# DMA transposes in place of TensorE transposes for the normalised activations, and the Fourier mixer in its channel-first order

## The reference

```
for l in 0, 1:
    h = rmsnorm(x, mix_norm_g[l])                 # over the 1024 channels of a position
    x = x + (even_mixer if l == 0 else odd_mixer)(h)
    h = rmsnorm(x, ffn_norm_g[l])
    x = x + (silu(h @ w_gate[l]) * (h @ w_up[l])) @ w_down[l]      # 1024 -> 2816 -> 1024
out = rmsnorm(x, final_norm_g)

odd_mixer(h):
    z = h @ w_in                                  # 1024 -> 1536
    c, u, v = z[:512], gelu(z[512:1024]), gelu(z[1024:])
    yc = per head of 128 channels: real(fft2(c, axes=(positions, channels), ortho)) @ fourier_w[head]
    yd = u * (spatial_w @ layernorm(v) + b)       # in chunks of 128 positions
    return concat(yc, yd) @ w_out
```

## Time and profile before

| | |
|---|---|
| time of three runs | 3428.40, 3431.67, 3632.03 us; median 3431.67 |
| profiled execution | 3428.40 us, its span on the slowest core (core 6) 3426.9 us |
| busy in the span | PE 2912.4 us (85%), DVE 987.9 (29%), ACT 833.8 (24%), POOL 310.7 (9%) |
| mixer 0: norm / projection / pooling / convolution / output | 0 to 106 / to 312 / to 366 / to 624 / to 741 us |
| feed-forward 0 | 742 to 1759 us |
| mixer 1: norm / projection / gating / Fourier / output | 1761 to 1857 / to 1976 / to 2177 / to 2281 / to 2395 us |
| feed-forward 1 | 2396 to 3427 us |

### The profile page before, as it was taken

One profiled execution on the slowest core, in us unless ns is written; L12 is line 12 of the kernel. 1 busy time (PEld: TensorE's weight loads), 2 busy tenths in 40 slices (PEclk: granted clock), 3 DMA queues, 4 the chain that ended last, 5 costly groups with the idle time before them and its releaser, 6 DMA issues.

```text
span 3426.9 us, 42073 instructions; the slowest of 8 cores (3407.2 to 3426.9 us)
## 1 busy us (share of the span) xinstructions
PE 2912.4 (85%) x14392; PEld 1376.4 (40%) x14392; DVE 987.9 (29%) x1566; ACT 833.8 (24%) x1515; POOL 310.7 (9%) x337
## 2 busy tenths in 40 slices
PE   2875999877999999999955966299599899899898
PEld 2433544333444444444433422164244444444444
DVE  5342322341122132221135044153212323323222
ACT  5211344111112211111025345230212212212211
POOL 0000122000101101101000033200110010010000
PEclk9987999988999999999976976599799999999999
DMA  8002000689645635536254000438965465454432
GB/s 217 26 1 34 2 1 1 205 264 165 81 120 103 81 136 88 86 114 81 53 157 157 30 1 1 101 114 286 208 87 110 113 76 122 105 74 123 80 50 80
DMA packets 259436, 336.74 MB, mean 98 GB/s; under 512 B 10784, under 2 KB 199840, under 8 KB 258464
## 3 DMA queue, kind: packets, MB, share of 16 engines
q0 software_dynamic: 196448, 117.62, 25.9%
q1 hardware_dynamic: 62784, 216.43, 18.5%
HBM read 380.31 MB, written 71.30 MB: 132 GB/s over the span
## 4 chain that ended last, share of the span: by engine, by line
PE 79%; DMA 7%; ACT 4%; DVE 4%; issue 4%; POOL 1%; DVEq 0%; SPq 0%; ACTq 0%; POOLq 0%
PE ps L111 79%; DMA sb_wgu<-ffn_w_up 3%; ACT sb_junk L298 2%; DMA sb_xin<-xres 2%; DVE sb_diag L546 1%; DMA sb_fw<-od_fourier_w 1%; ACT sb_vt L803 1%; DVE sb_hb L308 1%; DMA sb_xin<-x 1%; POOL sb_vt L807 1%; DMA sb_band<-band 1%; POOL sb_vn L810 1%; DVE sb_bst L781 0%; ACT sb_vt L775 0%; DMA xres<-sb_xout 0%
## 5 line engine op out<-in xcount | busy, mean ns | idle before, releaser
L111 PE MATMUL ps<-sb_h2T,sb_wgu 128*128 128x512 bf16 x5632 | 1237.6, 383 | 46.9 <-DMA sb_wgu<-ffn_w_up 46.9
L111 PEld LDWEIGHTS ps<-sb_h2T,sb_wgu 128*128 128x128 bf16 x5632 | 556.0, 99 | 725.4 <-issue 74.7
L111 PE MATMUL ps<-sb_wd,sb_gT 128*128 128x512 bf16 x2816 | 613.0, 379 | 10.8 <-DVE sb_gT L432 10.8
L432 DVE TENSOR_TENSOR sb_gT<-sb_tmp,ps 128x512 bf16<-128x512 f32 x352 | 242.1, 688 | 1041.2 <-PE ps L111 1023.6
L111 PE MATMUL ps<-sb_w_in,sb_bigA 128*128 128x512 bf16 x1792 | 426.6, 402 | 51.7 <-DVE sb_p_sb L560 35.7
L430 ACT ACTIVATE sb_tmp<-ps 128x512 f32<-128x512 f32 x352 | 210.1, 597 | 1027.4 <-PE ps L111 1027.3
L111 PEld LDWEIGHTS ps<-sb_wd,sb_gT 128*128 128x128 bf16 x2816 | 273.9, 98 | 339.2 <-issue 14.5
L111 PE MATMUL ps<-sb_ident,sb_hb 128*128 128x128 bf16 x1024 | 114.6, 281 | 237.5 <-DVE sb_hb L308 110.2
L111 PEld LDWEIGHTS ps<-sb_w_in,sb_bigA 128*128 128x128 bf16 x1792 | 180.2, 102 | 280.6 <-issue 89.0
L119 POOL DMA_DIRECT2D sb_wgu<-ffn_w_gate x88 | 77.6, 882 | 1978.4 <-PE ps L111 1643.3
L298 ACT ACTIVATE sb_junk<-sb_xin 128x1024 bf16<-128x1024 f32 x128 | 134.3, 1049 | 357.8 <-DMA sb_xin<-xres 347.3
(11 more groups left out here) (101 smaller groups left out, 1375.8 us busy)
## 6 DMA issues: line engine op xcount, KB each, us to landing
sb_xin<-xres SPq DMA_DIRECT2D x192, 512.0 KB, 5.5
xres<-sb_xout SPq DMA_DIRECT2D x96, 512.0 KB, 3.7
sb_wgu<-ffn_w_gate POOLq DMA_DIRECT2D x88, 512.0 KB, 6.4
sb_wgu<-ffn_w_up POOLq DMA_DIRECT2D x88, 512.0 KB, 8.3
sb_xin<-x SPq DMA_DIRECT2D x64, 512.0 KB, 5.7
out<-sb_xout SPq DMA_DIRECT2D x32, 512.0 KB, 3.0
sb_wd<-ffn_w_down POOLq DMA_DIRECT2D x4, 2816.0 KB, 73.8
sb_gbc<-norm_g SPq DMA_DIRECT2D x11, 512.0 KB, 4.4
```

The source lines that it names most:

```text
L111: ins = self.nc.tensor.matmul(o, lhsT=l, rhs=r, start=st, stop=sp)
L432: k.op(dve, lambda e: e.tensor_tensor(out=gT[:, j, tg * 512:(tg + 1) * 512], in0=tmp[:, ts_, :], in1=ps[:, bu, :], op=ALU.mult), reads=[d_ ...
```

## The change

Two things change together. (1) The transpose step of `norm_stages` is one DMA issued by SP that reads `hb` and writes the transposed tile into `hT`; the eight matmuls and the two PSUM copies go. The factor sqrt(1024) is put on the gain by one DVE instruction per call. Every tile of `hT` and `h2T` gets a DMA semaphore of its own. (2) The Fourier mixer runs channels first: c is made channel-major and stays in SBUF as `cT` (no `cdr`, no `ctm`); per head the channel DFT with `fourier_w` (64 matmuls, 16 copies to Q), a transpose on TensorE (64 matmuls, 16 copies to Q2), a complex 32-point DFT (128 matmuls, 16 copies to Y), and the position DFT (64 matmuls, 8 copies). All are of 128 columns. Q, Q2 and Y have one buffer each, without the parity of the head.

```diff
@@ -283,6 +282,9 @@
             gbc, xin, hb, junk = io.gbc, io.xin, io.hb, io.junk
             d_gbc, d_xin, d_hb, d_junk = io.d_gbc, io.d_xin, io.d_hb, io.d_junk
             k.dma(sp, [(gbc[:, 0, :], T["norm_g"][gidx])], writes=[d_gbc[0]], semdep=d_gbc[0])
+            k.op(dve, lambda e: e.tensor_scalar(out=gbc[:, 0, :], in0=gbc[:, 0, :], scalar1=float(np.sqrt(D)),
+                                                scalar2=None, op0=ALU.mult),
+                 reads=[d_gbc[0]], writes=[d_gbc[0]])
...
@@ -312,18 +314,9 @@
 
             def s_tr(i):
                 h_ = stt[i]["h"]
-                b = k.banks(2, pool=bpool)
-                psv = ps[:, b:b + 2, :].rearrange("p b (c n) -> p (b c) n", n=128)
-                k.mm([(psv[:, kk, :], hb[:, h_, kk * 128:(kk + 1) * 128], ident[:], True, True)
-                      for kk in range(8)],
-                     reads=[d_hb[h_], d_ident], writes=[psd[b], psd[b + 1]])
                 c0 = col0 + i * 128
-                k.op(act, lambda e: e.activation(out=hT[:, 0:4, c0:c0 + 128], in_=psv[:, 0:4, :], func=AF.Copy,
-                                                 scale=float(np.sqrt(D))),
-                     reads=[psd[b]], writes=[hT_deps[i]])
-                k.op(dve, lambda e: e.tensor_scalar(out=hT[:, 4:8, c0:c0 + 128], in0=psv[:, 4:8, :],
-                                                    scalar1=float(np.sqrt(D)), scalar2=None, op0=ALU.mult),
-                     reads=[psd[b + 1]], addw=[hT_deps[i]])
+                k.dma(sp, [(hT[:, :, c0:c0 + 128], hb[:, h_, :])], reads=[d_hb[h_]],
+                      writes=[hT_deps[i]], semdep=hT_deps[i], transpose=True)
...
-                d_h2T = [[Dep() for _ in range(8)] for _ in range(2)]
+                d_h2T = [[k.dmadep() for _ in range(8)] for _ in range(2)]
...
-                d_hT = [Dep() for _ in range(NT)]
+                d_hT = [k.dmadep() for _ in range(NT)]
...
+                cT = sb(ms, nc, "cT", [128, 4, S], BF16)
...
+                    nev = [0]
...
+                    def epi_c(tg, c, bl):
...
+                            k.op(act, lambda e: e.activation(out=cT[:, c, tg * 512:(tg + 1) * 512], in_=ps[:, bl[0], :],
+                                                             func=AF.Copy),
+                                 reads=[psd[bl[0]]], writes=[d_cT[c]])
...
+                    proj_fm(w_in, d_w, [[c * 128] for c in range(4)], bigA, lambda tg: d_hT[tg * 4:(tg + 1) * 4], 8, epi_c)
...
+                    m12 = sb(s1, nc, "m12", [128, 4, 2, 128], BF16)
+                    Q = sb(s1, nc, "Q", [128, 2, 32, 32, 4], BF16)
+                    Q2 = sb(s1, nc, "Q2", [128, 2, 32, 128], BF16)
+                    Y = sb(s1, nc, "Y", [128, 2, 32, 128], BF16)
...
-                        for sl, src_, sg in ((0, 0, 1), (1, 1, -1), (2, 1, 1), (3, 0, 1), (4, 1, -1), (5, 0, -1)):
-                            k.op(act, lambda e: e.activation(out=m3[:, h, sl, :], in_=ps[:, b, src_ * 128:(src_ + 1) * 128],
-                                                             func=AF.Copy, scale=float(sg * sc)),
-                                 reads=[psd[b]], writes=[d_m12])
+                        k.op(act, lambda e: e.activation(out=m12[:, h, 0, :], in_=ps[:, b, 0:128], func=AF.Copy,
+                                                         scale=float(sc)),
+                             reads=[psd[b]], writes=[d_m12])
+                        k.op(act, lambda e: e.activation(out=m12[:, h, 1, :], in_=ps[:, b, 128:256], func=AF.Copy,
+                                                         scale=float(-sc)),
+                             reads=[psd[b]], writes=[d_m12])
...
+                    d_Q = [[Dep() for _ in range(8)] for _ in range(2)]
+                    d_Y = [[Dep() for _ in range(8)] for _ in range(2)]
...
+                        for bb in range(0, 32, 4):
+                            for r in range(2):
+                                b = k.banks(1)
+                                k.mm([(ps[:, b, i * 128:(i + 1) * 128], cT[:, h, (bb + i) * 128:(bb + i + 1) * 128],
+                                       m12[:, h, r, :], True, True) for i in range(4)],
+                                     reads=[d_cT[h], d_m12], writes=[psd[b]])
+                                evac_on(r, Q[:, r, :, bb:bb + 4, :].rearrange("p c b j -> p b c j"),
+                                        ps[:, b, :].rearrange("p (i c j) -> p i c j", i=4, j=4),
+                                        [psd[b]], [d_Q[r][bb // 4]])
+                        for ri in range(2):
+                            for cg0 in range(0, 32, 4):
+                                b = k.banks(1)
+                                k.mm([(ps[:, b, i * 128:(i + 1) * 128],
+                                       Q[:, ri, cg0 + i, :, :].rearrange("p b j -> p (b j)"), ident[:], True, True)
+                                      for i in range(4)],
+                                     reads=d_Q[ri] + [d_ident], writes=[psd[b]])
+                                evac_on(ri, Q2[:, ri, cg0:cg0 + 4, :].rearrange("p c a -> p (c a)"), ps[:, b, :],
+                                        [psd[b]], [d_Q2[ri][cg0 // 4]])
+                        for cg0 in range(0, 32, 4):
+                            for r in range(2):
+                                b = k.banks(1)
+                                mms = []
+                                for i in range(4):
+                                    mms.append((ps[:, b, i * 128:(i + 1) * 128], Q2[:, 0, cg0 + i, :],
+                                                fab[:, 0, r * 128:(r + 1) * 128], True, False))
+                                    mms.append((ps[:, b, i * 128:(i + 1) * 128], Q2[:, 1, cg0 + i, :],
+                                                fab[:, 1, r * 128:(r + 1) * 128], False, True))
+                                k.mm(mms, reads=[d_Q2[0][cg0 // 4], d_Q2[1][cg0 // 4], d_fab], writes=[psd[b]])
+                                evac_on(r, Y[:, r, :, cg0 * 4:(cg0 + 4) * 4].rearrange("p b (i j) -> p i b j", i=4),
+                                        ps[:, b, :].rearrange("p (i b j) -> p i b j", i=4, j=4),
+                                        [psd[b]], [d_Y[r][cg0 // 4]])
...
                         for b0 in range(0, 32, 4):
                             b = k.banks(1)
                             mms = []
                             for i in range(4):
...
+                                mms.append((ps[:, b, i * 128:(i + 1) * 128], Y[:, 0, b0 + i, :], gcs[:, 0, b0 + i, :], True, False))
+                                mms.append((ps[:, b, i * 128:(i + 1) * 128], Y[:, 1, b0 + i, :], gcs[:, 1, b0 + i, :], False, True))
+                            k.mm(mms, reads=d_Y[0] + d_Y[1] + [d_gcs], writes=[psd[b]])
+                            evac_on(h % 2, yv[:, b0:b0 + 4, :], ps[:, b, :].rearrange("p (b a) -> p b a", b=4),
                                     [psd[b]], [d_yTf[h * 8 + b0 // 4]])
```

More of the change, by code:

```diff
@@ L114, in mm, with dma @@
         return ev
-    def dma(self, q, pairs, reads=(), writes=(), semdep=None):
+    def dma(self, q, pairs, reads=(), writes=(), semdep=None, transpose=False):
         self._pre(q, reads, writes)
         for (o, i) in pairs:
-            ins = q.e.dma_start(out=o, in_=i)
+            ins = q.e.dma_start(out=o, in_=i, transpose=True) if transpose else q.e.dma_start(out=o, in_=i)
             semdep.semval += 16
@@ L178, in make_consts @@
     ang = 2 * np.pi * np.outer(b, b) / 32.0
[L179 to L183, removed]
+    Cr = np.cos(ang)
+    Ci = -np.sin(ang)
+    I4 = np.eye(4)
+    FA = np.concatenate([np.kron(Cr, I4), np.kron(Ci, I4)], axis=1)
+    FB = np.concatenate([np.kron(-Ci, I4), np.kron(Cr, I4)], axis=1)
+    c["fab"] = np.stack([FA, FB], axis=1).astype(np.float32)
     a = np.arange(128)
     sp = (32 * a[None, :] + b[:, None])
-    a = 32 * (a % 4) + a // 4
     th = 2 * np.pi * (a[:, None, None] * sp[None, :, :]) / 4096.0
@@ L220, in build @@
     xres = nc.dram_tensor("xres", [S, D], F32, kind="Internal").ap()
-    cdr = nc.dram_tensor("cdr", [S, 512], BF16, kind="Internal").ap()
     dump_t = {}
@@ L695, in mixer1 @@
                 bigA = sb(ms, nc, "bigA1", [128, 8, S], BF16)
-                d_hT = [Dep() for _ in range(NT)]
-                d_cdr = k.dmadep()
+                cT = sb(ms, nc, "cT", [128, 4, S], BF16)
+                d_hT = [k.dmadep() for _ in range(NT)]
+                d_cT = [Dep() for _ in range(4)]
                 d_yTv = [Dep() for _ in range(NT)]
@@ L720, in mixer1 @@
                     k.dma(pool, [(swT[:], T["od_spatial_wT"])], writes=[d_swT], semdep=d_swT)
[L722 to L732, removed]
-                        else:
[L734 to L738, removed]
+                    nev = [0]
+                    def epi_c(tg, c, bl):
+                        nev[0] += 1
+                        if nev[0] % 2:
```

(34 more changed lines are left out.)

8 lines of the change are left out of this document (2 added, 6 removed).

## The result

The changed kernel takes 3547.97 us (median of 3 runs, 3546.62 to 3548.61) against 3431.67: ratio 1.0343 (1.0313 to 1.0373), slower. The forecast was 3454, a loss of 22 us, with a range to 3780; the measured loss is 116 us. The two profiled spans, 3426.9 and 3547.0 us, differ by 120.1, and that is what has to be found. Some executions here run a die at a lower clock and take longer, and the ratios compare the others alone.

The account below looks back on a forecast made before the run. The prediction took TensorE as the bound (79% of the chain of waits), with DMA the fuller resource in the norms. Its terms, 11 + 10 + 10 - 39 + 30 = +22 us, gave a median of 3454 us; range 3390 to 3780.

Parts of the forecast that it names:

- The price c: One DMA transpose of a 256 KB tile: 1.33 us of transfer, 2.4 us to landing, ends 0.77 and 4.6.
- Steps 1 and 2: Norms of mixers 0 and 1: 32 added transposes each, DMA at share 1.06; +11 and +10 us.
- Step 3: First eight tiles of each feed-forward layer: transposes delay the weights, half of 10 us assumed; +5 us each, +10 together.
- Step 4: Six joints between a down projection and the next gu: without transpose copies the add runs sooner; 6.5 us each, -39.
- Step 5: Fourier mixer: more matmuls and copies on the path, 22.4 us per head; +30 us, between +20 and +45.
- Slow transposes: Mainly both norms: DMA is the fuller resource, a transpose costs over 1.86 us; 3555 at 2.5, 3774 at 4.6; chance 31%.

Follow-up runs that it names:

- te_start: The changed kernel with TensorE transposes and PSUM copies for the first eight tiles of each feed-forward layer; ratio 1.0230, near 3511 us.
- weights_after: The changed kernel with POOL's weight loads of each feed-forward layer held back until the eight transposes have landed; one run, 3522.6 us.
- joints_again: The kernel before with DMA transposes only inside the down projections; ratio 0.9939.
- copies_in_fours: The changed kernel with the position-DFT copy walked in another order, writing runs of four bf16; ratio 1.0166, 3489 us.

## Why the prediction was wrong, point by point

- *The price c.* Near in the joints: the last three transposes of each hold SP for 1.26 to 1.57 us and land 3.1 to 3.8 us after their issue, against 1.33 and 2.4. Wrong as one number for all stretches. The estimate of 1.0 us from the Trainium skill ("DMA: Bandwidth & Descriptors", section "Latency and other measured facts") is a fifth below the shortest hold in these traces, 1.22 us. The 1309 ns per block of the Trainium skill ("VectorE: DVE Perf Modes", section "The three transpose paths") times eight, 10.5 us, does not hold for one DMA of eight blocks in a quiet stretch, where 3.0 us to landing is the shortest.
- *Steps 1 and 2, norms, +11 and +10*: measured +10.4 and +12.5, at the DMA share of 1.07 for the 1.06 assumed. The size is right, but by luck: the steps had DMA too full over the whole norm, and the trace has all of the loss in the first four tiles, +12 and +15 us beside POOL's weights, with the other tiles 2 to 6 us faster than before. It is the mechanism that step 3 missed; no run holds these weights back, so for the norms this rests on the place of the loss. Two details were off: the low clock at the start of the projection cost 0.9 us and not 2 (the first 49 matmuls took 13.5 us, before 12.6), and DVE did wait for `hb`, 95.5 us in the two norms together, since a transpose landed after 5.3 us and not 2.4.
- *Step 3, layer starts, +5 each*: +27.9 and +25.2. **This step failed.** I asked what the transposes would do to POOL's weights, found from the Fourier stage that SP's traffic slows POOL's little, and took half of 8c / 1.06. The reverse was not asked: what POOL's stream does to a transpose. It stretches it from 1.5 to 9.3 us, which PE's 22 us of cover cannot take. te_start and weights_after showed it.
- *Step 4, joints, -39*: -18 and -21 by the trace, with PE stopping after 16 matmuls. Right; alone, in joints_again, they gave 15 and 18.
- *Step 5, Fourier, +30*: +77. **This step failed too, and it was the larger part.** The wait for `fourier_w` fell by 8.7 us, just past the end of the bound that I gave. The heads, 98 us by my working, took 153. I had counted the copies, their engine and their order rightly (copies_in_fours gives 97), but took 0.52 and 0.62 us for all of them from copies that write runs of four; the changed position-DFT copy writes single bf16 values 64 bytes apart. The sentence "if copies to strided Q and Y take a fifth longer" looked at the wrong tiles: Q and Y write runs of four and cost 0.60 to 0.63 us on ACT and 0.69 on DVE.
- *The rivals.* Slow transposes had 31% and named the right direction, but not the place: in the median a transpose held SP for less than its deciding point of 1.86 us wherever SP had the engines to itself or shared its own queue, and for more only beside another queue. Of the 120 us, about 56 are the scattered copies, 43 more than foreseen are the starts of the layers, and the other 21 are near the 22 of the sum.

## What to carry to other kernels

A DMA that is made of many small packets has no one price: cost it in each stretch beside the queue that runs there, and in both directions. When a copy is moved or rewritten, compare the write runs of the new access pattern with those of the row from which its duration is taken. And try the order before the mechanism: statistics ahead of the add gave the joints back with either kind of transpose.
